# More large products in the chunk loops and in front of the first pair of a woven RWKV recurrence

## The reference, cut to what matters

```
proj = rmsnorm(x, norm1_g) @ w_in                   # [512, 1792 rwkv + 2304 attention + 2048 gates]

def wkv7_scan(r, w, k, v, a, b, reverse):           # 8 heads of 64, forward and backward
    def step(S, inp):                               # S: [64, 64] for each head
        sa = einsum('bhij,bhj->bhi', S, a_t)
        S = S * w_t[:, :, None, :] + sa[..., None] * b_t[:, :, None, :] + v_t[..., None] * k_t[:, :, None, :]
        return S, einsum('bhij,bhj->bhi', S, r_t)

for d, reverse in enumerate((False, True)):
    decay = exp(-exp(-softplus(-(w_decay0[d] + tanh(xw) @ w_decay_up[d])) - 0.5))
    a = sigmoid(a_gate0[d] + xa @ a_gate_up[d])
    kd = heads(k * (1.0 + (a - 1.0) * k_a))
    wkv = wkv + wkv7_scan(rh, heads(decay), kd, vh, -kk, kk * ah, reverse)
```

## Time and profile before

| | us |
|---|---|
| median of three executions | 3168.64 |
| the profiled execution, its own time | 3169.78 |
| its span in the profile | 3168.0 |
| TensorE busy with matmuls | 2805.0 (89%) |
| TensorE busy with weight loads | 2053.2 (65%) |
| VectorE busy | 1449.4 (46%) |
| ScalarE busy | 880.8 (28%) |
| landing of a 512 KB tile of ada, from its issue, median | 4.2 |
| landing of a 512 KB tile of w_in, median | 3.8 |

### The profile page before, as it was taken

How to read it: one execution, slowest core, us unless ns; L and a number is a source line. 1 busy time by engine, 2 the same in 40 slices (tenths; PEclk the granted TensorE clock), 3 DMA queues, 4 the chain that set the end, 5 groups by cost and what they waited for, 6 DMA issues and landing times.

```text
span 3168.0 us, 48322 instructions
## 1 busy us (share of the span) xinstructions
PE 2805.0 (89%) x21116; PEld 2053.2 (65%) x21116; DVE 1449.4 (46%) x2739; ACT 880.8 (28%) x1432; POOL 118.0 (4%) x197
## 2 busy tenths in 40 slices
PE   6799999998868777783898899999988988999999
PEld 5577777775653332331776677888876666778887
DVE  5554646556551010014466655433356665553433
ACT  3322131313410000002233453322223335432231
POOL 0010101010000000001000000000000000000000
PEclk9899999999978899996999999999999999999999
DMA  4243535353258999994324322333332332323332
GB/s 133 67 152 121 158 102 162 101 155 143 93 234 331 428 428 427 429 428 165 96 82 98 100 89 78 97 100 97 96 85 77 96 77 90 110 80 100 94 99 80
DMA packets 152265, 489.53 MB, mean 155 GB/s; under 512 B 13168, under 2 KB 40432, under 8 KB 139632
## 3 DMA queue, kind: packets, MB, share of 16 engines
q1 hardware_dynamic: 113824, 365.52, 32.3%
q0 software_dynamic: 25840, 94.12, 9.2%
q10 hardware_dynamic: 12384, 26.74, 2.6%
HBM read 456.44 MB, written 29.90 MB: 154 GB/s over the span
## 4 chain that ended last, share of the span: by engine, by line
PE 69%; DVE 12%; DMA 12%; ACT 5%; issue 1%; SPq 0%; POOL 0%; DVEq 0%; ACTq 0%; POOLq 0%
PE psum L156 66%; DMA wslot<-in_w_up 4%; DMA wslot<-in_w_gate 3%; DMA wslot<-in_w_down 3%; PE psum L159 3%; DVE halfL L165 2%; DVE sc__234 L195 1%; ACT halfH L162 1%; DVE m L192 1%; DVE a20S L180 1%; DVE a21S L180 1%; ACT a1S L162 1%; ACT L162 0%; DVE n_xn L168 0%; DVE n_ht L168 0%
## 5 line engine op out<-in xcount | busy, mean ns | idle before, releaser
L165 DVE TENSOR_TENSOR halfL<-ring,halfH 128x1024 fp32r<-128x1024 f32 x302 | 367.5, 1221 | 718.1 <-ACT halfH L162 717.6
L162 ACT ACTIVATE halfH<-ring 128x1024 fp32r<-128x1024 f32 x302 | 316.6, 1053 | 742.6 <-PE psum L156 740.7
L156 PE MATMUL psum<-hH,halfH 128*128 128x512 f32 x1200 | 487.0, 406 | 9.7 <-DVE halfL L165 9.6
L156 PE MATMUL psum<-hL,halfH 128*128 128x512 f32 x1200 | 474.4, 395 | 0.0
L156 PE MATMUL psum<-hH,halfL 128*128 128x512 f32 x1200 | 474.2, 395 | 0.0
L156 PE MATMUL psum<-wslot,XT 128*64 128x512 f32 x1024 | 259.2, 665 | 76.7 <-DMA wslot<-in_w_gate 42.3
L156 PEld LDWEIGHTS psum<-hH,halfH 128*128 128x128 f32 x1200 | 229.2, 191 | 84.9 <-issue 24.0
L156 PEld LDWEIGHTS psum<-hH,halfL 128*128 128x128 f32 x1200 | 229.1, 191 | 49.7
L156 PEld LDWEIGHTS psum<-hL,halfH 128*128 128x128 f32 x1200 | 229.4, 191 | 44.2
L156 PEld LDWEIGHTS psum<-wslot,XT 128*64 128x64 f32 x1024 | 90.4, 152 | 244.7 <-issue 243.5
L156 PE MATMUL psum<-halfH,hH 128*128 128x512 f32 (+2 forms) x576 | 219.3, 381 | 11.8 <-DVE halfL L165 8.4
(11 more groups left out here) (438 smaller groups left out, 3887.4 us busy)
## 6 DMA issues: line engine op xcount, KB each, us to landing
wslot<-in_w_gate SPq DMA_DIRECT2D x32, 2048.0 KB, 29.8
wslot<-in_w_up SPq DMA_DIRECT2D x32, 2048.0 KB, 29.6
wslot<-in_w_down SPq DMA_DIRECT2D x32, 2048.0 KB, 30.1
ring<-in_w_in SPq DMA_DIRECT2D x120, 512.0 KB, 3.8
ada<-in_w_ada POOLq DMA_DIRECT2D x96, 512.0 KB, 4.2
ring<-in_w_gu SPq DMA_DIRECT2D x88, 512.0 KB, 3.6
ring<-in_w_down SPq DMA_DIRECT2D x44, 512.0 KB, 3.8
gate_rows<-stage ACTq DMA_DIRECT2D x48, 256.0 KB, 2.1
```

The costliest lines, as they stand in the source:

```text
L156: return self.e.matmul(*a, **k)
L162: return self.e.activation(*a, **k)
L165: return self.e.tensor_tensor(*a, **k)
```

## The change

```
@@ recurrence_order @@
+        for _ in range(6):
+            yield from more()
         for x in ("squares", "sums", "root"):
             yield "kk", 0, x
@@
-                if (i - 4) * 18 // 26 > (i - 5) * 18 // 26:
+                if (i - 4) * 11 // 26 > (i - 5) * 11 // 26:
                     yield from more()
@@
-                    if pr < 3:
+                    for _ in range(2 - part if pr < 3 else 0):
                         yield from more()
```

## The result

The changed kernel took 3179.41 us (median of seven, 3177.47 to 3182.64), the kernel before, beside it, 3168.39. The ratio is 1.0044 with a 95% interval of 1.0033 to 1.0054: 10 to 17 us longer. A second comparison, made later, gave 1.0040 (1.0023 to 1.0057). The forecast was 3176, slightly slower than before, by 7.4 us. Sign and range held. The size was low, and not every term came out as written.

The account below looks back on a forecast made before the run. TensorE was taken as the bound almost throughout. Rows −47.7, loops +32.6, arow cover +6.4, VectorE steps +3.0, ada tiles +2.2 and front +10.9 gave +7.4 us: 3176 us, range 3158 to 3188.

Parts of the forecast that it names:

- A second burst in a loop: Chunk loops: each added burst costs 1.36 us on TensorE's path, 32.6 us for 24.
- The arow cover: Rows at i = 13: without its burst TensorE waits for ScalarE's arow copies; 6.4 us given back over four pairs.
- Front: Before pair 0's rows: a later split delays VectorE's work, 9.9 us longer, plus 1.0 of low clock.
- the half at 150.65: Front: ScalarE's half of the split at n = 5 ends at 150.65 us, and VectorE waits for it.
- up to 4 us less: Front, lower bound: if the clock comes back before the value products, the front costs up to 4 us less.
- sign for a free front: Sign of being wrong: pair 0's first turned products before 163 us would mean the front is free.
- ada tiles in pair 3: Rows, through the end of pair 3: tiles late where steps without a burst follow each other; 2.2 us over all pairs.
- starts from its end and shifts with it: Attention, merge and experts, behind the recurrence, only shift with its end; no cost of their own.
- Low clock in the rows: Start of pair 0's rows: one more low-clock step than before, 1.0 us.
- the shift at i = 8 and 17 of the rows: Rows: VectorE's moved norming and scaling delay TensorE at these steps, 3.0 us together, between 0 and 6.
- low clock into pair 0's rows: Rival: after the nearly idle front the clock stays low some 20 us into these rows; +16.1, 3185 us, chance 0.20.
- The free front: Rival: front (but for 2.4 us) and cover cost nothing; −12.7, 3156 us, chance 0.15.

Follow-up runs that it names:

- the one with slot 13: The changed kernel with the rows' burst at i = 14 moved to i = 13 in all four pairs; ratio 1.0029 against the kernel before.
- the late tail: The changed kernel with pair 3's eight bursts and last spill spread to i = 30; ratio 1.0031 against the kernel before.
- the move alone: The kernel before with no front bursts, chunk loops doubled, fewer row slots (i = 13 kept, fifteen slots in pair 3); ratio 1.0015 against the kernel before.

## Why the prediction was right, and where it was not

That sign and range held is in part luck. Against the forecast the stages miss by −3.9 (front), +2.9 (rows of pairs 0 to 2), +3.5 (loops), +7.5 (rows of pair 3) and −3.1 (to the scores), together +6.9. The waits of TensorE listed for 165 us on rose from 11.3 to 25.7 us, 14 more where 9 to 13 were named.

**Right in mechanism and size.** A second burst in a loop: two take 2.94 us where one takes 1.59, 1.35 for 1.36; loop 0 without low clock grew by 58.97 − 46.75 = 12.2, of which 8 × 1.36 = 10.9 are bursts, 0.7 is an arow wait of the last ada group and the rest is put down to where VectorE's mark stands. The Trainium skill (TensorE: Matmul & The Clock Gate, "Wait — 56ns, not 53.3ns?") has 215.7 ns for a matmul of 512 columns; the loop shows 1.35 / 6 = 225, so the row that was taken stands. This is the price of a burst read locally; for the sum over a whole stage see the shift of the list below. The arow cover: 6.4 forecast. At i = 13 TensorE waits 1.69, 1.69, 1.10 and 1.69, and keeping the slot gives 4.9 back in three pairs, of which about 1.5 is a low stretch less. Not foreseen there: the same kind of wait, 0.66, ahead of two loops. Before, TensorE waited 0.49 us for VectorE a product earlier in that place, behind a split that has moved, and this hid the arow copies. Mrb: 5.0 for 3.4, as forecast small.

**Front: right mechanism, a term too large.** The prediction had the half at 150.65 and the first Aa at 168.7, 18.05 us later. The trace has 145.59 and 162.72 to 163.47, 17.9 later. So the chain on VectorE is right to 0.2 us, and the half is what came earlier: the clock was back ahead of the value products, so that Vn starts at 141.55 instead of 146.6. That is the "up to 4 us less" of the text, and not a matter of this kernel alone. With the return at 134 to 137 us before stands at 154.8 and after at 163.1 to 163.5, a price of 8.4; with the return at 144 before stands at 159.7 and a changed kernel (the one with slot 13) at 166.6, a price of 6.9. Forecast: 9.9. The prediction took the one clock that its profile had for a property of the kernel. Its sign for a free front, turned products before 163 us, lay only 0.1 to 0.5 us below what an early return gave: a mark in time cannot be such a sign unless the return is named with it. Its text put the start of all this in the place of the splits, and the runs bear that out. First turned products by the number of bursts ahead of the key's squares:

| bursts in front | clock back at 134 to 137 | clock back at 144 |
|---|---|---|
| none | 154.82 | 159.71, 159.67 |
| four | 155.13, 155.28 | |
| six | 163.07, 163.35, 163.47, 163.63 | 166.62 |
| eight | 159.27, 159.47 | 161.80 |

Six cost 8.4 and 6.9 us, eight 4.5 and 2.1, four 0.4.

**The failed term: ada tiles in pair 3, 1.0 forecast.** The step that failed, though sign and range held, is the one on what lies behind: everything behind the recurrence "starts from its end and shifts with it; pair 3's loop and the attention have no bursts before or after". With bursts ending at i = 23, SP's next loads are let out 13 us earlier (693.50 for 706.79) and meet the ada tiles. Rows of pair 3: −4.2 where −11.7 was forecast. Spreading the bursts took 7.0 us out of these rows. Every kernel in which q and k were issued ahead of the last ada tile has such a wait in pair 3's rows (2.4 to 4.9 us, or 1.7 and 1.5 with eight in front and doubled loops, where another of 1.5 stands ahead of these loads) with tiles of full size, and none of those in which they were issued behind it has one (before in both profiles, the late tail, four and eight in front of the kernel before: the last tile at 703.49 and q at 706.79, or 708.73 and 712.02). The forecast's count of steps without a burst priced POOL's way round and never asked what SP would send into the same engines. The other side of this coin was missed too: the stretch to the scores is 3.1 shorter. The loads no longer run beside pair 3's loop, and the idle stretch of 1.9 us in it is gone; that the loads are the cause is argued from their place.

**Low clock in the rows, 1.0 forecast.** In pairs 0 to 2 the rows hold 3.4 and 3.1 us of low clock before, 7.1 and 17.1 after. At the low level half of each is lost: 4.4 us more on the mean, 3.4 more than forecast, which is all of the step from −23.4 to −20.5. Nor does it stand where the forecast put it, at the first turned products: there the clock was back at 164. Two stretches recur in both profiles of the changed kernel: at 184 behind the Mrb wait of 2.14 us, and at 197 behind the arow wait of 1.69. The others move from one execution to the next, and this part stays a mean over two.

**Not in the sum: the shift of the list behind the front.** Rows and loops of pairs 0 to 2 are best taken together, since VectorE's mark between them moves. They took 452.7 and 454.3 us before, and 465.8 with only six bursts in front, though each stage there has as many bursts as before: 12.3 us more, above the 8.8 of that front. About 2.6 of it is low clock and about 7 more waits of TensorE (SA 4.0, arow 2.0, 1.2 more for Mrb). The forecast priced the shift at i = 8 and 17 of the rows and nowhere in the loops. In the changed kernel the same stretch took 15.7 us more than before (466.4 and 472.0) where +9.2 was forecast. And doubling the loops without any shift made it 6.8 longer clear of low clock, where 24 × 1.36 − 21 × 1.59 gives −0.8. So no run shows the gain of 0.23 us for each burst moved from rows to loops in a whole kernel, although the local price shows it.

The rival "low clock into pair 0's rows" was wrong in its cause: the low clock that set in at 156 to 157 was over at 164, with the first turned products, in both profiles of the changed kernel, where the rival needed 10 us of it. The time, 13 to 14 us above before by the ratios, lies between the forecast's +7.4 and this rival's +16.1. The free front (−12.7) is refuted by both profiles.

Open: what takes the gain of the doubled loops. Of the 7.6 us by which the move alone misses its two terms, 4.8 are more waits of TensorE (only 1.2 of them for ada tiles); the rest is not traced. Whether the doubling pays once the tiles come in time is open too: a third buffer for them would tell, and it was not tried.

## What to carry to other kernels

When work is taken out of a stretch, list what that work was let run ahead of, on every queue: the transfer behind it starts sooner and may meet one that was never late. Where engines follow one list, moving an item changes the place of every later one (here a 1.2 us split at every fourth burst), and the place of the split costs more than the number of bursts: six in front cost 7 to 8 us, eight 2 to 5, four next to nothing. Such a shift is paid in the later stages too, so price them all. And take two profiles of the kernel before where a clock level carries part of the sum.

## What the runs showed of the hardware

- The same program has the granted clock back at 134 us in one execution and at 144 in another, which moves its recurrence by 4.9 us, while the timed ratio of the two is 0.9996.
- Behind the Mrb wait of 2.1 us and the arow wait of 1.7 us in pair 0's rows a stretch with 3.4 us of low clock followed in both profiles of the changed kernel; behind the arow wait of 1.7 us in pair 1 it followed in one of the two. Such a stretch cost a full loop about 1.55 us.
- A 512 KB tile that lands in 4.2 us as a rule took 9.7 when two loads of 1536 KB were issued within 0.9 us ahead of it, though it came on another queue (408 GB/s, DMA share 1.03).
- While or shortly after the loads of q, k and v filled the DMA engines, TensorE stopped for 1.6 to 2.5 us inside a group of matmuls, with no semaphore to wait for. It is in pair 3's loop of the five profiles in which the q load was issued some 5 us ahead of the copy of `bon` (the kernel before twice, the late tail, four and eight in front of the kernel before), and in none of the others. What it waits for, the profile does not show. One candidate was not tested: in four of these stops a packet of the DMA queue that the page calls `instruction` lies within a microsecond ahead of the idle time (720.5 to 721.0, idle from 721.1, and 724.0 to 724.5, idle from 724.7, in the two profiles of the kernel before; 723.0 to 723.6, idle from 723.7, and 729.4 to 729.7, idle from 729.6, in the late tail).
